# Expert blocks of 32 tokens on four column tiles, a ring of twenty weight slots

## The reference, cut to what matters

```python
logits = xt @ w_router + b_router                 # 512 tokens, 32 experts
top_vals, top_idx = lax.top_k(logits, 4)          # each token goes to 4 experts
top_gates = softmax(top_vals)
# for each block of tokens xb of one expert e:
gate = minimum(xb @ w_gate[e] + b_gate[e], 7.0)   # 1024 x 1024
up = clip(xb @ w_up[e] + b_up[e], -7.0, 7.0)      # 1024 x 1024
y = (gate * sigmoid(1.702 * gate) * (up + 1.0)) @ w_down[e] + b_down[e]
out = segment_sum(y * gate_of_the_token)          # back to the tokens
```

## Time and profile before

| | us |
|---|---|
| median of three runs | 3245.41 |
| the profiled execution: its time | 3249.86 |
| its span | 3248.2 |
| routing, from 1938 to 1983 | 45 |
| experts, from 1983 to 3204 | 1221 |
| final stage, from 3204 | 44 |

### The profile page before, as it was taken

How to read it: one execution, slowest core, us unless ns; L and a number is a source line. 1 busy time by engine, 2 the same in 40 slices (tenths; PEclk the granted TensorE clock), 3 DMA queues, 4 the chain that set the end, 5 groups by cost and what they waited for, 6 DMA issues and landing times.

```text
span 3248.2 us, 35773 instructions
## 1 busy us (share of the span) xinstructions
PE 2914.8 (90%) x12968; PEld 1749.5 (54%) x12968; DVE 1303.7 (40%) x2101; ACT 741.9 (23%) x1042; POOL 111.8 (3%) x171
## 2 busy tenths in 40 slices
PE   6997889999899989999897687899998999998984
PEld 5775668887677658787585273233332333332221
DVE  6874656664673644333475623111111111111113
ACT  3633332122463333122332111000000000000001
POOL 0020000000000000000010000000000000000002
PEclk7999999999999999999998788999999999999997
DMA  7273236664223022332231019775599989979995
GB/s 227 78 233 104 69 117 178 200 181 121 81 78 91 1 78 83 92 105 72 79 95 39 0 46 353 296 296 217 185 402 410 410 316 388 410 306 410 410 410 196
DMA packets 392996, 638.63 MB, mean 197 GB/s; under 512 B 28404, under 2 KB 278388, under 8 KB 392904
## 3 DMA queue, kind: packets, MB, share of 16 engines
q1 hardware_dynamic: 374792, 590.77, 50.8%
q0 software_dynamic: 9376, 31.14, 2.7%
q10 hardware_dynamic: 8736, 15.47, 1.4%
HBM read 610.78 MB, written 26.54 MB: 196 GB/s over the span
## 4 chain that ended last, share of the span: by engine, by line
PE 71%; DVE 8%; DMA 7%; SPq 6%; ACT 5%; issue 3%; POOL 0%; ACTq 0%; DVEq 0%; another core or an unknown queue 0%
PE bank L2148 24%; PE bank L189 12%; PE bank L190 12%; PE bank L191 12%; SPq L2038 5%; DMA ring<-w_down 4%; DMA ring<-w_gate 2%; PE bank L2153 1%; PE bank L868 1%; PE bank L869 1%; SPq L281 1%; PE bank L2140 1%; PE bank L909 1%; DVE WLO L162 1%; DVE x2t L2250 1%
## 5 line engine op out<-in xcount | busy, mean ns | idle before, releaser
L2148 PE MATMUL bank<-ring,xT 128*64 128x512 f32 x3200 | 718.0, 596 | 42.8 <-DMA ring<-w_up 21.6
L189 PE MATMUL bank<-HH,WHI 128*128 128x512 f32 x1360 | 548.9, 404 | 69.7 <-DVE HL L549 38.1
L190 PE MATMUL bank<-HL,WHI 128*128 128x512 f32 x1360 | 535.6, 394 | 0.0
L191 PE MATMUL bank<-HH,WLO 128*128 128x512 f32 x1360 | 535.0, 393 | 0.0
L2148 PEld LDWEIGHTS bank<-ring,xT 128*64 128x64 f32 x3200 | 220.4, 137 | 490.0 <-issue 386.0
L2148 PE MATMUL bank<-ring,hT 128*64 128x512 f32 x1600 | 361.9, 597 | 28.0 <-DMA ring<-w_down 26.2
L162 DVE TENSOR_TENSOR WLO<-RAW,WHI 128x2048 fp32r<-128x2048 f32 (+1 forms) x133 | 282.9, 2127 | 147.6 <-ACT WHI L154 147.4
L189 PEld LDWEIGHTS bank<-HH,WHI 128*128 128x128 f32 x1360 | 258.7, 190 | 144.4 <-issue 34.9
L154 ACT ACTIVATE WHI<-RAW 128x2048 fp32r<-128x2048 f32 (+1 forms) x133 | 236.3, 1777 | 261.9 <-PE bank L191 193.0
L191 PEld LDWEIGHTS bank<-HH,WLO 128*128 128x128 f32 x1360 | 258.9, 190 | 55.1
L190 PEld LDWEIGHTS bank<-HL,WHI 128*128 128x128 f32 x1360 | 259.7, 191 | 53.2 <-issue 3.1
(11 more groups left out here) (388 smaller groups left out, 2970.2 us busy)
## 6 DMA issues: line engine op xcount, KB each, us to landing
ring<-w_gate SPq DMA_DIRECT2D x128, 1024.0 KB, 11.4
ring<-w_up SPq DMA_DIRECT2D x128, 1024.0 KB, 13.8
ring<-w_down SPq DMA_DIRECT2D x128, 1024.0 KB, 15.9
RAW<-w_ffn_in SPq DMA_DIRECT2D x88, 512.0 KB, 5.3
RAW<-w_ada SPq DMA_DIRECT2D x40, 1024.0 KB, 5.3
RAW<-w_in SPq DMA_DIRECT2D x37, 1024.0 KB, 5.6
RAW<-w_ffn_out SPq DMA_DIRECT2D x32, 704.0 KB, 4.8
expert_results<-ysb ACTq DMA_DIRECT2D x102, 128.0 KB, 5.5
```

What stands on the lines that cost most here:

```text
L189: pe.matmul(out, lhi, rhi, start=start, stop=False)
L190: pe.matmul(out, lhi, rlo, start=False, stop=False)
L191: return pe.matmul(out, llo, rhi, start=False, stop=stop)
L2148: ins = pe.matmul(out[halves(h), :], xT[:, k % 4, halves(k // 4)], m["ring"][:, c, at:at + 512], start=False, stop=k == KD - 1)
```

## The change

Blocks have 32 tokens (`BLK`), and each expert has at least two (`LEAST`). A product keeps 32 tokens on a quarter of TensorE's columns and streams 256 columns; four column tiles hold the four quarters of the result. Tokens are gathered as 128 rows of a quarter token, and a block's result is one store whose rows are cut into four pieces of 1 KB. The tiles in SBUF between them (`xg`, `xT`, `gc`, `th`, `uc`, `hh`, `hT`, `ysb`) have 256 columns instead of 512.

The ring has 20 slots in five groups of four; `ring_group` gives the group of each expert's gate, up and down. The experts are written out: TensorE has, for each of the 32, the first block as code of its own, and a loop for the further ones, whose bounds are the ends of the experts' blocks in registers. SP issues 12 loads per expert with fixed addresses, each behind a wait for the last block of the expert that had the slot, and behind the landing of the load before on the same semaphore. It has loaded expert 0, and gate and up of expert 1, ahead of the loop. `bei`, `bed`, `fresh` and `freshd` are gone; `ends` and `count` are new. The bias rows are loaded by ScalarE's queue instead of SP's.

```diff
-BLK = 64
-MAXB = S * TOP // BLK + EXPERTS
+BLK = 32
+TILES = P // BLK
+COLS, DEEP = D // TILES, KD // TILES
+LEAST = 2
+MAXB = S * TOP // BLK + LEAST * EXPERTS
 MIN_BLOCKS = S * TOP // BLK
+ZEROED = 64 // BLK
...
-MOE_SLOTS = 12
+RING, RING_GROUPS = 20, 5
...
+def ring_group(e, w):
+
+    return (3 * e + w + 2) % RING_GROUPS
...
-        sp.wait_ge(*mix.event("terms"))
-        sp.dma_start(m["bp"][:].rearrange("r (w n) -> r w n", w=3), W["terms"].rearrange("w r n -> r w n")).then_inc(*sg.inc("ro_bp", also=[("bp", None)], n=16))
-
-        for c in range(MOE_SLOTS):
-            if c == MOE_SLOTS - 1:
+        for c in range(12):
+            if c == 11:
                 sp.wait_ge(*mix.event("logits"))
-            moe_load(sp, m, W, c, 0).then_inc(mo.sem["mo_first"], 16)
-        sp.wait_ge(mo.sem["mo_first"], 16 * MOE_SLOTS)
-        sp.wait_ge(*sg.event("bei"))
+            moe_load(sp, m, W, c, 0).then_inc(mo.sem[f"mo_raw{c}"], 16)
+        for c in range(8):
+            if c == 4:
+                sp.wait_ge(*sg.event("tokens"))
+                sp.wait_ge(*sg.event("stored"))
+            sp.wait_ge(mo.sem[f"mo_raw{c}"], 16)
+            moe_load(sp, m, W, c, 1).then_inc(mo.sem[f"mo_raw{c}"], 16)
+        sp.wait_ge(*sg.event("count"))
         return
...
+        act.wait_ge(*mix.event("terms"))
+        act.dma_start(m["bp"][:].rearrange("r (w n) -> r w n", w=3), W["terms"].rearrange("w r n -> r w n")).then_inc(*sg.inc("ro_bp", also=[("bp", None)], n=16))
...
+        v.tensor_scalar(m["nbf"][:], m["nbc"][:], float(LEAST), None, ALU.max).then_inc(*sg.inc("ro_dve", also=[("nbc", None)]))
...
+        v.tensor_scalar(nb, nb, float(LEAST), None, ALU.max).then_inc(*sg.inc("ro_step"))
...
-        v.tensor_copy(m["bei"][:, 0:NB], be[0:1, 0:NB])
-        v.tensor_copy(m["bed"][:, 1:NB + 1], be[0:1, 0:NB])
-        v.memset(m["bed"][:, 0:1], 0)
-
-        v.tensor_scalar(m["fresh"][:, 0:1], be[0:1, 0:1], 0.0, None, ALU.not_equal)
-        v.tensor_tensor(m["fresh"][:, 1:NB], be[0:1, 1:NB], be[0:1, 0:NB - 1], ALU.not_equal)
-        v.memset(m["freshd"][:, 0:1], 0)
-        v.tensor_scalar(m["freshd"][:, 1:2], be[0:1, 0:1], 0.0, None, ALU.not_equal)
-        v.tensor_tensor(m["freshd"][:, 2:NB + 1], be[0:1, 1:NB], be[0:1, 0:NB - 1], ALU.not_equal)
-        v.tensor_copy(m["bei"][:, NB:NB + 1], incl[0:1, 31:32]).then_inc(*sg.inc("ro_dve", also=[("bei", None)]))
+        v.tensor_copy(m["ends"][:], incl[0:1, :])
+        v.tensor_copy(m["count"][:], incl[0:1, 31:32]).then_inc(*sg.inc("ro_dve", also=[("count", None)]))
...
 def moe_load(sp, m, W, c, e):
+    name, a = MOE_CHUNKS[c]
+    w = W[f"w_{name}_2"][0][e].rearrange("(k p) n -> p k n", p=P)
+    slot = 4 * ring_group(e, c // 4) + a
+    return sp.dma_start(m["ring"][:, slot, :].rearrange("p (k n) -> p k n", k=2), w[:, 2 * a:2 * a + 2, :])
 
 
 def moe_sp(sp, sg, m, W, count):
 
+    end = lambda e: sp.value_load(m["ends"][0:1, e:e + 1], min_val=LEAST, max_val=MAXB)
+    two_back, one_back = None, end(0)
+    for e in range(1, EXPERTS):
+        for c, (w, a) in enumerate(MOE_CHUNKS):
+            if e == 1 and w != "down":
+                continue
+            if w == "gate":
+                sp.wait_ge(sg.sem["mo_up"], 4 * two_back + a + 1)
+            elif w == "up":
+                sp.wait_ge(sg.sem["mo_down"], 4 * two_back + a + 5)
+            else:
+                sp.wait_ge(sg.sem["mo_gate"], 4 * one_back + a + 1)
+            sp.wait_ge(sg.sem[f"mo_raw{c}"], 16 * e)
+            moe_load(sp, m, W, c, e).then_inc(sg.sem[f"mo_raw{c}"], 16)
+        two_back, one_back = one_back, end(e)
...
+    def store(i):
+        rows = W["ybuf"][bass.ds(i * BLK, BLK), :].rearrange("t (q d) -> q t d", q=TILES)
+        return act.dma_start(rows, m["ysb"][:])
...
+def moe_pe(pe, nc, sg, m, b, count):
     ident = m["K"][:, K_ID:K_ID + P]
+    tile = lambda q: slice(q * BLK, (q + 1) * BLK)
 
     def bias(out, sel, w):
 
+        for q in range(TILES):
+            pe.matmul(out[tile(q), 0:COLS], sel, m["bp"][:, w * D + q * COLS:w * D + (q + 1) * COLS], start=True, stop=False)
+
+    def products(e, c, out, xT):
+
+        pe.wait_ge(sg.sem[f"mo_raw{c}"], 16 * (e + 1))
+        a, slot = c % 4, 4 * ring_group(e, c // 4) + c % 4
+        for kk in range(2):
+            k = 2 * a + kk
+            for q in range(TILES):
+                at = kk * D + q * COLS
+                ins = pe.matmul(out[tile(q), 0:COLS], xT[:, k % DEEP, tile(k // DEEP)], m["ring"][:, slot, at:at + COLS], start=False, stop=k == KD - 1)
         return ins
 
     def turn(out, src):
+        for j in range(DEEP):
+            ins = pe.transpose(out[:, j * P:(j + 1) * P], src[:, j * P:(j + 1) * P], ident)
         return ins
 
+    def gate_up(e, i, done, first=False):
 
         pe.wait_ge(*sg.event("xT", loop=i, back=1))
         pe.wait_ge(*sg.event("sel", loop=i, back=1))
         pe.wait_ge(*sg.event("gc", loop=i, back=1))
         bias(b[0], m["sel"][:], 0)
+        for a in range(4):
+            products(e, a, b[0], m["xT"]).then_inc(*done("mo_gate", *["g"] * (a == 3)))
 
         pe.wait_ge(*sg.event("hT", loop=i, back=1))
         if first:
...
             pe.nop().then_inc(sg.sem["mo_pe"], 1)
         else:
             pe.wait_ge(*sg.event("hh", loop=i, back=1))
+            turn(b[6], m["hh"]).then_inc(*done("mo_pe", "hturned"))
         pe.wait_ge(*sg.event("gathered", loop=i))
+        turn(b[7], m["xg"]).then_inc(*done("mo_pe", "xturned"))
 
         pe.wait_ge(*sg.event("uc", loop=i, back=1))
         bias(b[1], m["sel"][:], 1)
+        for a in range(4):
+            products(e, 4 + a, b[1], m["xT"]).then_inc(*done("mo_up", *["u"] * (a == 3)))
+
+    def down(e, i, done):
 
         pe.wait_ge(*sg.event("ycopy", loop=i, back=1))
         pe.wait_ge(*sg.event("seld", loop=i, back=1))
         pe.wait_ge(*sg.event("hT", loop=i))
         bias(b[2], m["seld"][:], 2)
+        for a in range(4):
+            products(e, 8 + a, b[2], m["hT"]).then_inc(*done("mo_down", *["seld_used"] * (a == 0), *["y"] * (a == 3)))
+
+    def named(name, *keys):
+        return sg.inc(name, also=[(k, None) for k in keys])
+
+    def again(name, *keys):
+        return sg.sem[name], 1
+
+    _, ends = nc.values_load_multi_w_load_instructions(m["ends"][0:1, :], engines=[mybir.EngineType.PE], min_val=LEAST, max_val=MAXB)
+    for e in range(EXPERTS):
+        i = ends[e - 1] if e else 0
+        gate_up(e, i, again, first=not e)
+        if e:
+            down(e - 1, i, again)
+        with pe.Fori(i + 1, ends[e]) as i:
+            done = again if e else named
+            gate_up(e, i, done)
+            down(e, i, done)
...
+    at("ring", 36, [P, RING, SLOT])
```

More of the change, by code:

```diff
@@ L54 @@
 K_INV, K_I32, K_I48 = 774, 790, 822
-K_I64 = 892
-NK = 1020
+K_I64 = 952
+NK = 1080
 RAW_SLOTS, W_SLOTS = 4, 3
@@ L1965, in route_program @@
         v.memset(m["seld"][:], 0.0)
+        v.wait_ge(*sg.event("evac", 7))
         for k in range(KD):
-            v.tensor_scalar(m["n2x"][:, k % 4, k // 4 * BLK:(k // 4 + 1) * BLK], one[:, 0:BLK], vec[:, V2_N2 + k:V2_N2 + k + 1], None, ALU.mult)
+            v.tensor_scalar(m["n2x"][:, k % DEEP, k // DEEP * BLK:(k // DEEP + 1) * BLK], one[:, 0:BLK], vec[:, V2_N2 + k:V2_N2 + k + 1], None, ALU.mult)
         v.wait_ge(*sg.event("tokens"))
@@ L2046, in loads @@
[L2046 to L2070, removed]
@@ L2128, in moe_dve @@
                         ALU.is_equal).then_inc(*sg.inc("mo_dve", also=[("seld", None)]))
-def moe_pe(pe, sg, m, b, count):
+def moe_pe(pe, nc, sg, m, b, count):
     ident = m["K"][:, K_ID:K_ID + P]
-    def halves(h):
-        return slice(h * BLK, (h + 1) * BLK)
+    tile = lambda q: slice(q * BLK, (q + 1) * BLK)
     def bias(out, sel, w):
-        for h in range(2):
-            pe.matmul(out[halves(h), :], sel, m["bp"][:, w * D + h * 512:w * D + (h + 1) * 512], start=True, stop=False)
-    def products(c, out, xT):
-        a = MOE_CHUNKS[c][1]
-        for k in (2 * a, 2 * a + 1):
-            for h in range(2):
-                at = (k % 2) * D + h * 512
-                ins = pe.matmul(out[halves(h), :], xT[:, k % 4, halves(k // 4)], m["ring"][:, c, at:at + 512], start=False, stop=k == KD - 1)
+        for q in range(TILES):
[8 more added lines that the diff above has]
+                ins = pe.matmul(out[tile(q), 0:COLS], xT[:, k % DEEP, tile(k // DEEP)], m["ring"][:, slot, at:at + COLS], start=False, stop=k == KD - 1)
         return ins
     def turn(out, src):
-        for k in range(4):
-            ins = pe.transpose(out[:, k * P:(k + 1) * P], src[:, k * P:(k + 1) * P], ident)
-        return ins
-    def gate_up(i, first=False):
-        def done(key, *keys):
-            return (sg.sem["mo_pe"], 1) if first else sg.inc("mo_pe", also=[key, *keys])
+        for j in range(DEEP):
+            ins = pe.transpose(out[:, j * P:(j + 1) * P], src[:, j * P:(j + 1) * P], ident)
+        return ins
+    def gate_up(e, i, done, first=False):
```

(29 more changed lines are left out.)

93 lines of the change are left out of this document (42 added, 51 removed).

## The result

The changed kernel takes 3252.65 us (median of 20 runs, 3246.8 to 3260.2), the kernel before in the same session 3245.89 (20 runs, 3239.2 to 3249.4). The ratio is 1.0023, interval 1.0017 to 1.0029: slower by 6.8 us, where 19.6 were forecast. The time lies inside the forecast's range of 3195 to 3380 us.

The account below looks back on a forecast made before the run. TensorE and the weight loads were taken to bound the experts' stage in turn. Stage +2, expert ends +16 and routing +1 made +19 us, 3265 us from the median of 3245.4; range 3195 to 3380.

Parts of the forecast that it names:

- expert ends: Before the first block: TensorE loads 32 ends into registers with nothing hiding it, 8 to 25 us, taken as +16.
- TensorE's own time: Experts' stage: 92 blocks of 32 tokens take 1053 us against 1120 for 50 blocks of 64, 67 us less.
- loss to the feed: Experts' stage: TensorE's waits for weights go from 83 to 153 us, with gather and store at 1.82 us per block.
- the walks: Load-by-load count of TensorE's waits in the experts' stage: stage 1206 us after the change, 1204 before.
- TensorE's block: Experts' stage: one block of 32 tokens takes TensorE 11.45 us, with a product record each 53 ns.
- (b): Rival: TensorE's sequencer can't give a record per 53 ns; 3500 us at 68 ns, 3325 at 56; chance 0.24.
- (d): Rival: four column tiles run no faster than two, 21.9 us a block, 4070 us in all; chance 0.04.
- (a): Rival: the store runs on all 16 DMA engines, waits 98 us instead of 153, 3210 us in all; chance 0.24.
- (c): Rival: code fetches and stores meet on one DMA engine, waits 224 us instead of 153, 3336 in all; chance 0.10.
- at 150 us: Sign of the forecast: TensorE's waits for the ring of weight slots stand at 150 us.
- 36 packets per store: Sign of the forecast: queue q10 shows 36 packets for each store and not 48.
- The spacing of loads: Sign of the forecast: loads lie 2.9 us apart instead of 2.56 while two-block experts run.

Follow-up runs that it names:

- half_before: The kernel before with every ring load bringing only its first half, which both halves of the products read: 3153.6 us, ratio 0.9719 to the kernel before.
- half_after: The changed kernel with every ring load bringing only its first half, which both halves of the products read: 3094.7 us, ratio 0.9535 to the kernel before.
- store16: The changed kernel with the store of y as four transfers, each on sixteen DMA engines: 3218.1 us, ratio 0.9912 to the kernel before.
- store2: The changed kernel with the store of y as two transfers of outermost size 2, both on the same two engines: 3418.5 us, ratio 1.0531 to the kernel before.
- best1: The changed kernel with stores on sixteen engines, expert ends read earlier in two portions, and at least one block per expert: 3198.5 us, ratio 0.9857 to the kernel before.
- least1: The changed kernel with at least one block per expert instead of two, nothing else: 3221.3 us, ratio 0.9927 to the kernel before.

## Why the prediction came out as it did

Profiled executions, counted from the matmul with tri:

| term | forecast | measured | how |
|---|---|---|---|
| routing | +1 | +1.6 | the first transposes of xg come 25.37 us after it, before 23.75 |
| expert ends | +16 | +10.0 | from them to the first bias 12.47 us, before 2.47 |
| TensorE's own time | -67 | -73.6 | half_before to half_after |
| loss to the feed | +69 | +66.8 | 93.2 to 160.0 (the walks: 84 to 153) |
| final stage | 0 | +0.5 | 44.3 against 43.8 us |
| sum | +19 | +5.3 | medians: +6.8 |

The mechanism was the forecast one: TensorE's gain in the long experts is given back to the feed in the short ones, with the store on four engines. What failed is the size of two terms, the expert ends (+16, measured +10.0) and TensorE's own time (-67, measured -73.6). The two large terms nearly cancel, so errors of 6 us in each of these are most of the sum: the stage was to grow by 2 us and shrank by 6.8 (1221.7 to 1214.9). That the loss to the feed came out at +66.8 for +69 is in part luck, as below.

*The expert ends* ("one load and its check take 0.48+0.18+0.03 us, 8 to 25 us in all, I take 16"). The row was one load of one value. The 32 come in a single load of 2.157 us, and then 0.281 us each: 11.2 us. Nothing hid it, as forecast.

*TensorE's block* (11.45 us): 11.40, and the piece behind the last block takes 6.1 us instead of the 8.5 of before, which I had taken as equal. These are 4.2 and 2.4 of the 6.6 us missed; 0.05 us of a block is most of the measured difference, because it is counted 92 times. Rivals (b) and (d) are out: TensorE takes a product record each 54 ns for 91 us on end. (b)'s own sum was too dear: 208 x 0.054 + 1.5 would be 12.7 us for the 11.40 measured, so at the forecast's own pace its 1.5 us for waits and branch were already too much. The Trainium skill (TensorE: Matmul & The Clock Gate, "Wait — 56ns, not 53.3ns?") gives about 62 ns for a matmul with the hardware decode off. By that the block was estimated at 14.4 us, and the trace's 11.40 says that this bound isn't met here.

*The feed* (1.82 us per block, 153 us of waits). Two errors nearly cancel. By the landings the extra is (33.7 - 30.5)/2 = 1.6 us with the store on four engines, and (31.9 - 30.5)/2 = 0.7 with sixteen, where 12 x 16 packets of 0.159 us make the 30.5. For 1.5 the walk gives 135 to 139 us, not 160, for 0.73 98 to 103, not 130, and for the kernel before 83, not 93. The shortfall lies in the first late expert of a run: the walk had 5.8, 5.9, 7.0 and 5.9 us at experts 3, 10, 19 and 25, the trace has 10.3, 12.4, 13.2 and 12.6; the experts behind them agree within 2 us. What takes these 4 to 7 us of lead is open; the store's four engines don't explain it, since store16 falls short of its walk as well (130 for 98 to 103; the same experts lose 9.9, 7.3, 7.5 and 9.1 us there). The store's share was right in kind, and (a), with the store on sixteen engines, was priced 55 us below the forecast, where the chip gives 35. The Trainium skill (DMA: Bandwidth & Descriptors, "Why a DMA increments its semaphore by 16 and not by 1") gave the count of four, and adds that it is the lowest-numbered engines. Four closing packets a store, and the two transfers of store2 on the same two engines, agree.

*Code* (rival (c)): 107 transfers of 16 KB, 3.3 per expert for the forecast 3.4, and in the expert of eight blocks none from 2093 to 2166 us, over the last passes of its loop. They don't add up with the stores: on the same engines the feed would be 30.5 + 2 x 1.79 + 3.4 x 1.075 = 37.7 us, and it is 33.7.

*The signs.* Waits "at 150 us" was the wrong one to look for: the loss is 160, the table names 98. "36 packets per store" was a slip: the prediction's own 32 packets on each of four engines make 128 and 4, 132, as measured. The spacing of loads was to be 2.9 us and is 33.7/12 = 2.8, in store16 31.9/12 = 2.7.

## What to carry to other kernels

A store with outermost size 4 ran on four DMA engines, and every load that is spread over all sixteen waited for these four: count the closing packets of such a queue (4 a store here), and cut the store so that it uses all sixteen (32 rows outermost gave 16 closing packets a transfer and 35 us). Where a stage alternates between two bounds, a faster engine gains only in the stretches that it bounds; run both kernels with half the bytes, and the two shares stand apart at once. Work that fills waiting time (ten empty blocks, 114 us) is nearly free, and taking it out gains little (20 and 13 us of stage).

## What the runs showed of the hardware that was not expected

A taken branch over an expert's unused loop is dear. TensorE's sequencer in best1, and the timeline behind the first such branch:

```profile
L2210 PEldq COMPARE_BRANCH  x32: 68/77/6321, 1980.3 to 3112.3; - x32
```

```profile
1986.99 0.41 PE L2147 MATMUL bank<-bp,sel 96*32 96x256 bf16 x4 [5.28 <-issue]
```

```profile
PE bank L2147 <- issue: 54.7, 10, 9.4
```

The ten taken ones last 4.6 to 6.3 us each, the others 0.07 to 0.09, and TensorE stands still for 54.7 us in ten waits before the next bias; most of it must fall where the ring is late anyway, since the stage of best1 gains 12.8 us where the walk without these waits gives 14. The loop's way back, over as much code, shows no such wait. In each of the ten a code transfer of 16 KB starts 2.1 to 3.8 us behind the start of the branch and lasts 1.0 to 1.1 us, and in least1 it is the same. The Trainium skill (Runtime: NRT & Kernel Launch, "Instruction fetch mechanics") says that a taken branch to a page not yet held waits for its fetch; the trace agrees. The DMA engines are full at all ten (share 1.02 or 1.03), so whether the fetch is quicker beside fewer loads no run shows; it doesn't wait for all the loads issued before it, which take about 20 us to land in the changed kernel.
